# Two pieces of ScalarE's work change places in the attention stage of a two-block transformer kernel

## The reference

```python
# kind a: each query attends to the 128 keys of highest index score
score = einsum('bqh,bqhs->bqs', iw, relu(einsum('bqhd,bsd->bqhs', iq, ik)))
_, idx = lax.top_k(where(causal, score, -inf), n_top)          # n_top = 128
logits = einsum('bqgrd,bqkgd->bqgrk', q, k[idx]) * scale - slopes * dist
o_a = einsum(softmax(where(valid, logits, -inf)), v[idx])
# kind b: forgetting attention
logits = einsum('bqhd,bshd->bhqs', q, k) * scale + cum_q - cum_k
o_b = einsum(softmax(where(causal, logits, -inf)), v)
x = x + gate * (concat(rms_norm(o_a), rms_norm(o_b)) @ w_out)
```

## Time and profile before

| | |
|---|---|
| median of 3 runs | 2918.71 us (2918.24 to 2927.54) |
| the profiled execution | 2927.54 us, span 2925.8 us |
| granted TensorE clock, mean | 0.941 of full speed |
| busy | PE 91%, DVE 63%, ACT 36%, POOL 35% of the span |
| the changed stage | about 257 to 389 us of the span, 32 units |
| largest group | products L186 to L188, three of 660 to 673 us, not in this stage |

### The profile page before, as it was taken

One profiled execution on the slowest core, in us unless ns is written; L12 is line 12 of the kernel. 1 busy time (PEld: TensorE's weight loads), 2 busy tenths in 40 slices (PEclk: granted clock), 3 DMA queues, 4 the chain that ended last, 5 costly groups with the idle time before them and its releaser, 6 DMA issues. The chain is left out here.

```text
span 2925.8 us, 36529 instructions
## 1 busy us (share of the span) xinstructions
PE 2673.3 (91%) x13817; PEld 2176.6 (74%) x13821; DVE 1840.2 (63%) x3174; ACT 1065.9 (36%) x1682; POOL 1033.3 (35%) x494
## 2 busy tenths in 40 slices
PE   6897886989979999999997999999899979999999
PEld 3675774333357877778875899999899968888887
DVE  6958644111140627708855069998889967888888
ACT  2224642222332332126733333334455533333333
POOL 1223112222213334221132337887323233444442
PEclk8896897999969999998998999999999989999999
DMA  7730034999823434410042226787598799999995
GB/s 297 305 137 4 1 134 168 393 399 366 337 95 112 171 117 175 164 56 1 13 161 88 82 95 213 284 282 268 174 306 276 299 368 361 366 390 386 383 386 221
DMA packets 135610, 646.25 MB, mean 221 GB/s; under 512 B 21680, under 2 KB 22576, under 8 KB 91184
## 3 DMA queue, kind: packets, MB, share of 16 engines
q1 hardware_dynamic: 86512, 483.81, 44.1%
q0 software_dynamic: 48384, 158.38, 14.6%
q10 hardware_dynamic: 576, 2.27, 0.2%
HBM read 620.26 MB, written 75.50 MB: 238 GB/s over the span
## 5 line engine op out<-in xcount | busy, mean ns | idle before, releaser
L186 PE MATMUL psum<-h_hi,w_hi 128*128 128x384 f32 (+1 forms) x1808 | 672.9, 372 | 28.7 <-DVE h_lo L563 8.3
L187 PE MATMUL psum<-h_lo,w_hi 128*128 128x384 f32 (+1 forms) x1808 | 660.2, 365 | 0.0
L188 PE MATMUL psum<-h_hi,w_lo 128*128 128x384 f32 (+1 forms) x1808 | 659.0, 365 | 0.0
L167 POOL TENSOR_TENSOR w_lo<-ring,w_hi 128x2048 fp32r<-128x2048 f32 x64 | 302.8, 4731 | 744.7 <-ACT w_hi L160 704.6
L186 PEld LDWEIGHTS psum<-h_hi,w_hi 128*128 128x128 f32 x1808 | 347.6, 192 | 66.8 <-issue 24.3
L188 PEld LDWEIGHTS psum<-h_hi,w_lo 128*128 128x128 f32 x1808 | 346.5, 192 | 34.7
L187 PEld LDWEIGHTS psum<-h_lo,w_hi 128*128 128x128 f32 x1808 | 347.3, 192 | 33.4 <-issue 1.7
L2449 ACT ACTIVATE w_hi<-ring 128x2048 fp32r<-128x2048 f32 x127 | 242.5, 1910 | 219.8 <-PE psum L188 200.9
L186 PE MATMUL psum<-w_hi,a_hi 128*128 128x512 f32 x768 | 301.8, 393 | 19.5 <-DVE a_lo L2934 13.4
L187 PE MATMUL psum<-w_lo,a_hi 128*128 128x512 f32 x768 | 300.5, 391 | 0.0
L188 PE MATMUL psum<-w_hi,a_lo 128*128 128x512 f32 x768 | 300.4, 391 | 0.0
(11 more groups left out here) (483 smaller groups left out, 4633.9 us busy)
## 6 DMA issues: line engine op xcount, KB each, us to landing
ring<-in_weights SPq DMA_DIRECT2D x199, 1024.0 KB, 6.3
w_expert_in<-in_experts_in SPq DMA_DIRECT2D x32, 2048.0 KB
hid_dram<-hid_acts SPq DMA_DIRECT2D x64, 384.0 KB
gates_dram<-block_gates SPq DMA_DIRECT2D x24, 1024.0 KB
hid_tiles<-hid_dram SPq DMA_DIRECT2D x64, 384.0 KB
gate_tiles<-gates_dram SPq DMA_DIRECT2D x15, 1536.0 KB, 12.1
o<-in_ada_later SPq DMA_DIRECT2D x16, 1024.0 KB, 5.8
w_expert_down<-in_experts_down SPq DMA_DIRECT2D x16, 1024.0 KB
```

Of the source, the lines that this page charges most:

```text
L167: k.nc.gpsimd.tensor_tensor(lo, slot(k, n), hi.bitcast(F32), ALU.subtract).then_inc(k.w_ready, 1)
L186: k.nc.tensor.matmul(out, hi, x_hi, start=start, stop=False)
L187: k.nc.tensor.matmul(out, hi, x_lo, start=False, stop=False)
L188: return k.nc.tensor.matmul(out, lo, x_hi, start=False, stop=stop)
```

## The change

In ScalarE's loop over t, the block with `copy_turned(t - 2)` goes from ahead of `exp(t)` and the splits to behind them. `square(t - 4)` stays last. No instruction is added or taken out, no wait is changed, and the other engines' lists are the same.

```diff
                 for t in range(n + DEEP + 2):
-                    if 2 <= t < n + 2:
-                        copy_turned(t - 2)
                     if t < n:
                         exp(t)
                         p, i = units[t]
                         if i == 1 and p < len(pairs) - 1:
                             split(index_pairs + p + 1)
+                    if 2 <= t < n + 2:
+                        copy_turned(t - 2)
                     if t > DEEP + 1:
                         square(t - DEEP - 2)
```

## The result

| | before | after |
|---|---|---|
| median, on the first chip | 2919.2 us (4 runs) | 2942.3 us (4 runs) |
| ratio of the two | | 1.0062, 95% interval 1.0048 to 1.0078 |
| the same pair on another chip | 2922.0 us (23 runs) | 2942.8 us (6 runs) |
| ratio of the two | | 1.0067, 95% interval 1.0054 to 1.0079 |
| span of the profiled execution | 2925.8 us | 2934.3 us |

The change makes the kernel slower by 0.6 to 0.7%, some 19 us. The first ratio is that of the record, which has 18 executions of the changed kernel (median 2938.6 us); the table's median is of the first four of them, so the ratio isn't the quotient of the two medians. I had forecast 2928, + 9, and a range up to 2937. The direction was right; the size forecast was half of what came, and the result lies above the range.

What follows compares the result with a forecast made beforehand. VectorE was taken to bound the stage's first half, TensorE its second. Second half 6.9 + first half 1.6 + clock 0.8 = 9.3 us, on the median 2918.71 giving 2928 us (+0.3%); 8-in-10 range 2919 to 2937.

Steps and rivals of the forecast that it cites:

- What bounds each half: First block's attention: VectorE sets the pace from 286 to 328.6 us, TensorE is the bound from 343 to 389 us.
- The chain and its place: Second half: scores, maxima, exponentials, copy, transposes in sequence; TensorE stands 1.74 us after full-width units, transposes also late in the drain.
- The bare cost of the second half: Late copies cost 5.8 us over three pairs of heads and 1.1 us in the drain, 6.9 us together.
- The term for the splits: Second half, units with the next pair's two splits ahead of the copy: 0.27 us each, in two of three pairs.
- the copies of the other units: Second half, units of i = 0 and 2: moving their copies was put at no cost.
- The first-half term: First half, up to the maxima of unit 6: 1.6 us lost, bounds 0 and 3.0.
- the lower bound: First half: the delay costs 0 if the clock rises sooner and hides it.
- VectorE's wait at M(6): First half, maxima of unit 6: VectorE's wait was to grow by some 1.5 us in the profile after.
- The clock term: Second half: three idles of 1.74 us, half a fall of the clock taken, 0.8 us, bounds 0 to 4.8.
- rival (a): Second half: clock swings, half of TensorE's work at the low level, 2940 us, mean clock under 0.9; chance 0.10.
- The rest of the kernel: After the stage: nothing loads from memory during it, so its delay goes to the end one for one.

Runs made afterwards that it cites:

- e2: The changed kernel with the new order only in units t < 16, the old order from t = 16; 1.0004 of before.
- e1: The changed kernel with unread products filling TensorE's idle, six at three places and ten in the drain, copies still late; 2925.2 us, 1.0013 of before.
- e3: The changed kernel with the old order restored at the four 512-key units of the second half; 0.9985 of before.
- the second profile: The changed kernel run once more, nothing altered, beside later experiments on one chip; 1.0067 of before.
- e4: The kernel before, with TensorE also waiting for the 512-key units' exponentials at three places, idle 0.99 us each; 1.0013 of before.
- e5: The kernel before, with TensorE also waiting at three places for the squares after the 512-key units' exponentials; 2941.6 us, 1.0061 of before.
- e6: The kernel before, with fourteen unread products, started late, in TensorE's idle ahead of the masks of unit 16; 1.0001 of before.
- e7: e6 plus 28 unread float32 products at the start of the following norm, against the kernel before; 1.0012 of before.
- e8: The kernel before, with thirteen unread products from the start of TensorE's idle ahead of the masks of unit 16; 0.9993 of before.
- e9: e8 plus four unread products ahead of the last transposes in the drain, against the kernel before; 2919.7 us, 0.9985 of before.

## Why the prediction was wrong in size

- **What bounds each half: right.** The first half hides the change: it is 0.4 us longer than in before by the first profile, 0.1 shorter by the second, and 0.5 longer in e2.
- **The chain and its place: right.** TensorE waits for the copy behind the widest unit, for 1.57 us, three times, and 2.55 in the drain (forecast: T(18) 1.74 later, which it is, and T(30) 2.16 later, on top of 0.39, which makes the 2.55).
- **The bare cost of the second half: right.** Forecast 5.8 in the pairs and 1.1 in the drain; e1 shows 5.9 and 1.2. The term for the splits, 0.27, is there too: e1's maxima of 512 keys start at 343.50, 357.81, 372.16 and 386.16, so the two pairs with splits behind them take 14.31 and 14.35 us and the last 14.00. What I put at nothing, the copies of the other units, shows no idle of its own in the changed kernel; in e3 it is an idle of 0.23 us, and a pair takes 12.67 - 12.25 = 0.42 us more.
- **The first-half term, 1.6: wrong, but small.** At the place where I read it, M(6), it came out at - 0.2, and at M(16) at 0.4. Its steps hold up to W(2); then the clock rose sooner, the lower bound that I had named. The sign that I gave, VectorE's wait at M(6) some 1.5 us longer, failed: it waits 0.79 us, before 1.32.
- **The clock term, 0.8 with bounds 0 and 4.8: this is the step that failed.** It is 14.8 - 5.9 = 8.9 us in the pairs and 5.8 - 1.2 = 4.6 in the drain, 13.5 in all. It failed in three places. First, I took half a fall for three idles; every one brought a fall. Second, I priced a fall at 3.9 us of low clock, from a short one; here one lasts about 7 us (346.90 to 353.90) and costs 8.9 / 3 = 3.0 us, not 1.6. My own formula gives 7.0 x (1 - 1/1.70) = 2.9 for that length. Longer stretches stood in the trace of before: the 8.64 us behind the masks, in the same group of rows, and the same idle of 2.36 us a second time, with eight products behind it at the low clock (1.94 us, where the earlier trace rows has 1.08 for eight) and the eight transposes that follow still at it (1.89; the row is below the list). Third, I left the drain out: the longest of the new idles is there, 2.55 us, longer than the one of 2.36 that I had quoted for a fall. With the measured sizes of these three the sum is 6.9 + 0.4 + 3 x 3.0 + 4.6 = 20.9; it closes because the 3.0 and the 4.6 are what e1 leaves over, and the 2.9 above is the check of the first. How much of the 4.6 is the change's stays open, since the old order's drain falls too in five of eight profiles, for 3.5 us.
- **The rival (a), the clock that swings: it is what happened,** with a mean clock of 0.78, under the 0.9 that I had set as its mark. I gave it 0.10 and 2940, and argued against it from the idle of 1.16 us without a fall; e2 shows the same idle with one. The other argument, that TensorE stays above 85% busy, is true (41.08 of 46.00 us) and was no protection. The Trainium skill (TensorE: Matmul & The Clock Gate, A second HAM failure mode: psum-queue depth-cycling) warns of brief idles between groups of matmuls that make the clock swing. I read that as a thing that the trace bears out "only from 2.36 us up", though no idle between 1.16 and 2.36 at the high clock in this stage spoke for or against it. The changed kernel's trace agrees with it at 1.57 us, three times in three.
- **The rest of the kernel: as said.** The delay goes to the end; 20.9 us in the stage, 19.6 (15.8 to 23.1) in the runs.

The second idle of 2.36 us in the trace of before:

```profile
310.39 1.94 PE L743 MATMUL psum<-v_b,attn_probs_t 128*128 128x64 f32 x8 [2.36 <-DVE o L776]
```

A slip in the section on the change: the squares at the end of ScalarE's loop are those of unit t - 5, not t - 4. No term rests on it.

## What to carry to other kernels

When a change makes TensorE idle on a path where it is the bound, the idle is the smaller part of the bill: price the clock for every one, with the whole of the low stretch behind it, and leave it out only if idles of that length were seen to be harmless more than once. A copy that frees the only PSUM buffer belongs ahead of work that nobody waits for soon, however early that work's input is ready. If the idle can't be avoided, a few unread products in it can be worth more than they cost, provided that they end before the wait does.

## What the runs showed of the hardware

- Idles of 0.87 and 0.99 us, three of each in a row 14.3 and 13.4 us apart, left the granted clock at its high level; of 1.47 and 1.57 us, at places 17 us apart, all six (and three more in the second profile) brought it to the low one, for about 7 us each, though TensorE was busy without a gap right behind them.
- The idle of 1.16 us in the drain was followed by a fall in e2, e4, e5, e6 and e7 and by none in before, e3 and e8, with the same instructions. What ahead of it decides that isn't settled.
- M(0) to M(16) takes 69.3 to 69.9 us in eight profiles and 73.5 to 73.8 in e5, e8 and e9, the first of which has the old list there instruction for instruction. (The 73.3 and 73.4 of e6 and e7 are something else, the unread products in the time of the masks.) From 285 to 300 us the granted clock is 0.89 in before and 0.50 in e5 and e8 (below), so that TensorE, and no longer VectorE, is the bound there. Why isn't settled either. All six profiles with the new order in the first half are short, and three of the seven with the old are long: if that is more than chance, which wasn't tested, it would be a gain of the new order there, and a reason for e3's runs.
- The 31 executions of the kernel before beside e1 to e4 lay between 2911.4 and 2931.1 us. The larger part of such a scatter seems to lie outside this stage: outside it the 13 profiles differ by 13.0 us (2783.2 to 2796.2), while a long first half adds 4 us and a long drain 3.5.

The window of e8:

```profile
285.00:300.00 15.00, 14.67 (x70) 12.24 (x69) 12.34 (x35) 5.12 (x19) 0.00 (x0) 0.50 0.01 2
```
